# The state-space path of a hybrid encoder block: input tables on VectorE, one real prefix scan for the chunk states, output tables made late and kept in SBUF

## The reference, cut to what matters

```python
lam_bar = exp(lam * dt)                      # 64 groups x 64 complex states
b_bar   = ((lam_bar - 1) / lam)[..., None] * (b_re + 1j * b_im)
bu      = einsum('gpc,bsgc->bsgp', b_bar, u)             # 16 channels per group
states  = associative_scan(a_r*a_l, a_r*b_l + b_r)       # over 256 tokens
y = einsum('gcp,bsgp->bsgc', c_re, real(states)) - einsum('gcp,bsgp->bsgc', c_im, imag(states))
y = gelu(y + d_skip * u);  y = rmsnorm(y * sigmoid(y @ w_glu + b_glu))
```

## Time and profile before

| what | value |
|---|---|
| median of 3 runs | 1181.74 us (1181.29 to 1186.13) |
| profiled execution, its own time | 1184.79 us |
| its span, first to last instruction | 1182.9 us |
| PE busy | 1146.3 us (97%) |
| DVE busy | 743.5 us (63%) |
| ACT busy | 519.8 us (44%) |
| POOL busy | 174.9 us (15%) |
| mean granted TensorE clock | 0.985 |

### The profile page before, as it was taken

The page is one execution under the profiler, slowest core; times in us unless marked ns, Lnnn a source line. Parts: engine busy times, 40 slices in busy tenths (PEclk is TensorE's granted clock), DMA queues, the critical chain, the costliest instruction groups (busy, mean ns, idle before and its releaser), DMA issues.

```text
span 1182.9 us, 15345 instructions
## 1 busy us (share of the span) xinstructions
PE 1146.3 (97%) x5616; PEld 946.1 (80%) x5616; DVE 743.5 (63%) x844; ACT 519.8 (44%) x590; POOL 174.9 (15%) x197
## 2 busy tenths in 40 slices
PE   9879999899999999999999999999999999999996
PEld 6667778677898888888888888888888888888884
DVE  6999998764585565446465555546464555556465
ACT  6533343434574465343434344343434343343443
POOL 7464550884010000000000000000000000000000
PEclk9889899999999999999999999999999999999998
DMA  9577479869565656666666665666666665656652
GB/s 366 194 207 198 152 225 198 269 213 249 180 214 185 193 176 214 206 185 194 187 189 192 195 192 182 194 189 191 187 195 184 190 195 190 191 185 195 187 187 89
DMA packets 147401, 233.74 MB, mean 198 GB/s; under 512 B 25824, under 2 KB 46048, under 8 KB 146592
## 3 DMA queue, kind: packets, MB, share of 16 engines
q1 hardware_dynamic: 146432, 231.75, 64.8%
q0 software_dynamic: 640, 1.31, 0.5%
q10 hardware_dynamic: 288, 0.13, 0.0%
HBM read 223.82 MB, written 8.32 MB: 196 GB/s over the span
## 4 chain that ended last, share of the span: by engine, by line
PE 83%; DVE 8%; SPq 3%; DMA 3%; ACT 1%; issue 1%; POOL 1%; ACTq 0%; POOLq 0%; DVEq 0%
PE ps L1227 26%; PE ps L1229 25%; PE ps L1228 25%; DVE w_lo L746 3%; DMA raw<-in_w_in 3%; SPq L307 1%; DVE cl L887 1%; PE ps L1438 1%; SPq L344 1%; DVE cl_t L888 1%; PE ps L1507 1%; PE ps L1509 1%; PE ps L1508 1%; PE ps L1349 1%; PE ps L1306 1%
## 5 line engine op out<-in xcount | busy, mean ns | idle before, releaser
L746 DVE TENSOR_TENSOR w_lo<-raw,w_hi 128x1024 fp32r<-128x1024 f32 x384 | 486.4, 1271 | 403.0 <-ACT w_hi L468 402.1
L468 ACT ACTIVATE w_hi<-raw 128x1024 fp32r<-128x1024 f32 x384 | 407.0, 1061 | 643.8 <-PE ps L1229 545.2
L1227 PE MATMUL ps<-w_hi,actA_hi 128*128 128x512 f32 x576 | 230.2, 400 | 2.9 <-DVE w_lo L746 2.9
L1229 PE MATMUL ps<-w_hi,actA_lo 128*128 128x512 f32 x576 | 225.0, 391 | 0.0
L1228 PE MATMUL ps<-w_lo,actA_hi 128*128 128x512 f32 x576 | 224.8, 390 | 0.0
L1229 PE MATMUL ps<-w_hi,h2B_lo 128*128 128x512 f32 x352 | 137.0, 389 | 0.0
L1228 PE MATMUL ps<-w_lo,h2B_hi 128*128 128x512 f32 x352 | 136.9, 389 | 0.0
L1227 PE MATMUL ps<-w_hi,h2B_hi 128*128 128x512 f32 x352 | 136.9, 389 | 0.0
L1227 PEld LDWEIGHTS ps<-w_hi,actA_hi 128*128 128x128 f32 x576 | 108.5, 188 | 27.5 <-issue 4.9
L1229 PEld LDWEIGHTS ps<-w_hi,actA_lo 128*128 128x128 f32 x576 | 108.4, 188 | 23.0
L1228 PEld LDWEIGHTS ps<-w_lo,actA_hi 128*128 128x128 f32 x576 | 108.6, 189 | 20.6
(11 more groups left out here) (204 smaller groups left out, 1164.0 us busy)
## 6 DMA issues: line engine op xcount, KB each, us to landing
raw<-in_w_gate SPq DMA_DIRECT2D x88, 512.0 KB, 3.6
raw<-in_w_up SPq DMA_DIRECT2D x88, 512.0 KB, 3.7
raw<-in_w_down SPq DMA_DIRECT2D x88, 512.0 KB, 3.8
raw<-in_w_in SPq DMA_DIRECT2D x80, 512.0 KB, 5.5
raw<-in_w_out SPq DMA_DIRECT2D x32, 512.0 KB, 4.6
c_scratch<-cl SPq DMA_DIRECT2D x8, 512.0 KB, 3.4
y_tab<-c_scratch SPq DMA_DIRECT2D x8, 512.0 KB, 6.8
raw<-in_ssm_w_glu SPq DMA_DIRECT2D x8, 512.0 KB, 3.4
```

Of the source, the lines that this page charges most:

```text
L468: nc.scalar.activation(w_hi[:, s % SPL], raw[:, s % RAW], ACT.Copy).then_inc(S["high_done"], 1)
L746: tt(w_lo[:, s % SPL], raw[:, s % RAW], w_hi[:, s % SPL].bitcast(F32), ALU.subtract).then_inc(S["low_done"], 1)
L1227: mm(o, x_hi, h, start=first, stop=False)
L1229: return mm(o, x_lo, h, start=False, stop=last)
```

## The change

- The factor (lam_bar - 1)/lam is taken out of the input tables. `wb_table(b)` on DVE now uses the raw `b_re`, `b_im` (three 128x896 operations; ACT copies the ninth part), `bb` and `bbx` are gone, and `input_factors` multiplies the factor into the powers after the last input table, so that the output tables carry it.
- `angle_table`, `turn_tables` (ACT: four 128x1024 activations) make sines and cosines of each group's angle times the time chunk. `scan_states` turns the chunk inputs by them, does one real prefix scan with the moduli (`tensor_tensor_scan`, 128x1024) and `turn_back` turns back, per half of the groups. Each turn needs a copy with the halves swapped: `swap`, two DMAs of 256 KB, before the scan and again after it.
- The output tables `cl` are made later (`CL_AT` 31 to 60), stay in SBUF in three buffers and are read there by PE; only the in-chunk kernels go through DRAM (`k_table`: one store, its landing awaited, eight strips back into two buffers).
- `tables` is split: `wb_transposes` at `TR_AT`, `k_tables` at `K_AT`. The outputs come one batch at a time at chunks 39 to 70.
- POOL does no table and no scan any more; it issues the DMAs of the path (`u_local`, `swap`, `k_table`), which stood in SP's program before. `c_dram` and the second copy of u are gone.

```diff
-U_TR = (12, 21)
-CL_AT = (17, 19, 22, 25, 28, 31, 34, 37)
-TAB_AT = (16, 19, 25, 28, 31, 34, 37, 40)
-V_AT = tuple(t + 5 for t in TAB_AT)
-SCAN_AT = tuple(41 + 4 * k // 5 for k in range(NCH - 2))
+U_TR = (12, 19)
+WB_AT = (13, 15, 18, 20, 22, 24, 26, 28)
+TR_AT = (15, 17, 21, 23, 25, 27, 29, 31)
+V_AT = (18, 20, 24, 26, 28, 30, 32, 34)
+ANGLE_AT = (23, 27)
+TURN_AT = (26, 30)
+DECAYS_AT = (27, 34)
+FACTOR_AT = 29
+SCAN_AT = (30, 39)
+BACK_AT = (34, 42)
+CL_AT = (31, 35, 40, 45, 48, 53, 56, 60)
+K_AT = (33, 37, 42, 47, 50, 55, 58, 62)
+Y_AT = (39, 43, 48, 53, 56, 64, 67, 70)
-Y_AT = (64, 65, 67, 68, 70, 71, 73, 74)
-Y1T_MM = (70, 72, 77, 79)
+Y1T_MM = (68, 70, 73, 75)
...
+            def wb_table(b):
...
+                o, t = wb[b % 3][:, :, 1:], wb_t[:, :, 1:]
+                tt(o, of_groups(b_re, b, LOC - 1), of_powers(pr, b, 1, LOC - 1), ALU.mult)
+                link(tt(t, of_groups(b_im, b, LOC - 1), of_powers(pi, b, 1, LOC - 1), ALU.mult))
+                tt(o, o, t, ALU.add).then_inc(S["wb_ready"], 1)
...
+            def scan_states(h):
+                dve.wait_ge(d_swap[h], 32)
+                dve.wait_ge(S["turn_step"], 4 * h + 4)
+                dve.wait_ge(S["decays_ready"], h + 1)
+                x, y = (flat(z) for z in state_half(h))
+                tt(y, y, flat(sin[h][:]), ALU.mult)
+                link(tt(x, x, flat(cos[h][:]), ALU.mult))
+                link(tt(x, x, y, ALU.add))
+                nc.vector.tensor_tensor_scan(x, flat(decays[:]), x, 0.0, ALU.mult, ALU.add).then_inc(S["scanned"], 1)
+
+            def turn_back(h):
+                dve.wait_ge(S["scanned"], h + 1)
+                dve.wait_ge(d_swap_back[h], 32)
+                x, y = (flat(z) for z in state_half(h))
+                tt(y, y, flat(sin[h][:]), ALU.mult)
+                link(tt(x, x, flat(cos[h][:]), ALU.mult))
+                tt(x, x, y, ALU.subtract).then_inc(S["state_ready"], 1)
...
+            def k_table(b):
+                pool.wait_ge(S["kst_ready"], b + 1)
+                pool.dma_start(k_dram[b].rearrange("h p w -> p h w"), kst[:, b % 2]).then_inc(d_kst[b % 2], 16)
+                pool.wait_ge(d_kst[b % 2], 16 * (b // 2 + 1))
...
+                if b >= TBUF:
+                    pool.wait_ge(S["y_mm"], b - TBUF + 1)
+                for i in range(LOC):
+                    pool.dma_start(k_tab[i * CH:(i + 1) * CH, b % TBUF],
...
+            for h in range(2):
+                u_local(h)
+            for h in range(2):
+                pool.wait_ge(S["v_free"], HB * (h + 1))
+                swap(h, d_swap)
+            for h in range(2):
+                pool.wait_ge(S["scanned"], h + 1)
+                swap(h, d_swap_back)
+                k_table(h)
+            for b in range(2, 6):
+                k_table(b)
...
-                pe.wait_ge(S["v_free"], NB)
+                pe.wait_ge(S["y1_ready"], sum(bank == 7 for bank in Y_BANK))
```

More of the change, by code:

```diff
@@ L294, in build, with state_half, flat @@
         kst_w = kst[:].rearrange("p u h (d c) -> p u h d c", c=CH)
[L296 to L325, removed]
+        def state_half(h):
+            at = slice(HALF * h, HALF * (h + 1))
+            return state[:, at], swapped[:, at]
+        def flat(x):
+            return x.rearrange("p g k -> p (g k)")
         @block.sync
@@ new lines, in angle_table @@
+            def angle_table(h):
+                if h == 0:
+                    dve.wait_ge(S["uT_mm"], 2)
+                else:
+                    dve.wait_ge(d_uTst[1], 16)
+                c, s = cos[h], sin[h]
+                link(tt(c[:], scr[:, 2, HALF * h:HALF * (h + 1)].unsqueeze(2).to_broadcast([P, HALF, NCH]),
+                        vec[:, V_COUNT:V_COUNT + NCH].unsqueeze(1).to_broadcast([P, HALF, NCH]), ALU.mult))
+                link(ts(flat(s[:]), flat(c[:]), MAGIC, None, ALU.add))
+                stt(flat(c[:]), flat(s[:]), -MAGIC, flat(c[:]), ALU.add, ALU.subtract).then_inc(S["angles_ready"], 1)
@@ new lines, in wb_transposes @@
+            def wb_transposes(b, part):
+                if part == 1:
+                    pe.wait_ge(S["wb_ready"], b + 1)
+                    pe.wait_ge(S["wb0_ready"], b + 1)
+                    pe.wait_ge(S["u_copied"], 1 if TR_AT[b] < U_TR[1] else 2)
+                    if b:
+                        pe.wait_ge(S["wbT_ready"], b)
+                for g in range(4 * (part - 1), 4 * part):
+                    ins = tr(ps[:, 4 + g // 4, P * (g % 4):P * (g % 4 + 1)],
+                             wb[b % 3][:, g].rearrange("p d c -> p (d c)"), ident[:])
+                if part == 2:
+                    ins.then_inc(S["wb_mm"], 1)
@@ new lines, in k_tables @@
+            def k_tables(b):
+                pe.wait_ge(S["cl_ready"], b + 1)
+                if b == 0:
+                    pe.wait_ge(S["b_pad_ready"], 1)
+                else:
+                    pe.wait_ge(S["kpsum_free"], b)
+                for g in range(BG):
+                    h, q = divmod(g, 4)
+                    gg = BG * b + g
+                    ins = mm(ps[32 * q:32 * q + 32, 6, P * h:P * (h + 1)],
+                             b_re[:, gg:gg + 2].rearrange("p a c -> p (a c)"),
+                             cl[:, b % CBUF, g, 0:LOC].rearrange("p d c -> p (d c)"), start=True, stop=True)
+                ins.then_inc(S["k_mm"], 1)
@@ new lines, in y_batch @@
+            def y_batch(b):
+                pe.wait_ge(S["state_ready"], b // HB + 1)
+                pe.wait_ge(d_ktab[b % TBUF], 16 * LOC * (b // TBUF + 1))
+                if b:
+                    pe.wait_ge(S["y1_ready"], b)
+                else:
+                    pe.wait_ge(S["v_free"], NB)
+                if Y_BANK[b] == 6:
+                    pe.wait_ge(S["kpsum_free"], NB)
+                for a in range(2):
+                    at = slice(P * a, P * (a + 1))
+                    for q in range(4):
+                        mm(ps[32 * q:32 * q + 32, Y_BANK[b], at], u_loc[:, BG * b + 4 * a + q],
+                           k_tab[:, b % TBUF, 4 * a + q], start=True, stop=False)
+                    for q in range(4):
+                        ins = mm(ps[32 * q:32 * q + 32, Y_BANK[b], at], state[:, BG * b + 4 * a + q],
+                                 cl[:, b % CBUF, 4 * a + q, 1:].rearrange("p d c -> p (d c)"),
+                                 start=False, stop=True)
+                ins.then_inc(S["y_mm"], 1)
```

432 lines of the change are left out of this document (201 added, 231 removed).

## The result

The changed kernel takes 1189.66 us (median of 14 runs, 1186.29 to 1191.02) against 1183.68 us before (14 runs, 1181.29 to 1188.08). The ratio is 1.0043, with a 95% interval of 1.0032 to 1.0053 (it is worked out from all the runs and is not the ratio of the two medians, which would be 1.0051): slower, by about the 0.5% that the prediction called no change. Forecast were 1171.5 us and a range up to 1185. The profiled execution has a span of 1187.8 us, 4.9 us more than before.

What follows compares the result with a forecast made beforehand. TensorE bounds the kernel, busy 97%; chunks 0 to 79 lose 36 us, mostly to late VectorE. Old 36 less new losses 25.8 gives gain 10.2: 1184.8 to 1174.6, 1171.5 as a median, range 1161 to 1185.

Steps and rivals of the forecast that it cites:

- What goes away: Chunks 0 to 79: VectorE's operations turn short, losses at parameters, first `cl` and scans go; all of the old 36 us.
- Chunks 12 to 14: Chunk 12 starts in time, but `wb_table(0)` at 13 makes `low(14)` late for TensorE: loss 1.7 us.
- The way of u: Store and strips of u land at 66 us, TensorE wants them in chunk 18 at 63: loss 3, bounds 0 and 15.
- The scan, 2.4 us: Chunks 18 to 33: scan operation taken as two passes, VectorE's lead shrinks to about 1: loss 0.5 us, bounds 0 and 3.
- Chunk 34: TensorE idles after chunk 34 while VectorE awaits a queued swap: 12 us, bounds 11 and 15.5, plus 2.6 of slow clock.
- The output batches: From chunk 39, batches 0, 1 and 2 arrive late by 2.6, 1.6 and 0.6 us; slow clock beside these waits 1.2.
- Chunks from 80 on as before: From about chunk 80 only TensorE's own work counts and the change touches none of it: no difference there.
- rival 1: Output tables' strips land after 7 us instead of 3 in five batches: 1183 to 1186 us, no measurable change; chance 0.20.
- Rival 2: GpSimd's issue cost grows with a DMA's rows, 2.2 us each, first chunk inputs 15 us later: 1188 us; chance 0.10.
- Rival 3: Waits besides chunk 34 do not appear, u and strips land in time: gain 21 us, 1161 us; chance 0.12.
- The trap of GpSimd's issues: GpSimd's 80-odd DMA issues beside busy VectorE are not slowed; single-input passes of `angle_table` might add 1 us at most.

Runs made afterwards that it cites:

- e2: Kernel after the change with the first two batches of chunk inputs two chunks later (V_AT 20, 22 instead of 18, 20): 1180.80 us, ratio 0.9968 against before.
- e5: Kernel after the change with the first three output batches later (Y_AT begins 41, 44, 49 instead of 39, 43, 48): 1188.81 us, ratio 1.0027 against before.
- e3: Kernel after the change with small tiles moved so that matmul operands begin at multiples of 512 bytes in SBUF: 1181.97 us, ratio 0.9981 against before.
- e1: Kernel after the change with GpSimd issuing half 0's swap back before half 1's swap: 1174.32 us, ratio 0.9916 against before.

## Why the prediction was wrong, step by step

- *What goes away:* right. `w_lo` at 1.22 us, no VectorE operation of 3 us, no wait on the first `cl`, no new wait from chunk 54 on. (A slip of no consequence: 6 x 0.75 is 4.5 and not 4.4.)
- *Chunks 12 to 14:* nearly. Chunk 14 takes 3.97 us, 1.25 over 2.72, for a forecast loss of 1.7; another 0.9 is lost at chunk 10, which I did not see.
- *The way of u:* **mis-sized**, 3 us forecast, 9.1 measured (e2). The last strip landed at 67.7 us for a forecast 66, the smaller part of it, and that it came so close is luck: the store began at 49.5 for 51 and took 5.6 for 6.4, and the strips took 12.4 from first issue to last landing for 8.2. The larger part: I had taken one term of 1.2 us for the slow clock beside all waits but that of chunk 34, though the earlier trace rows had priced one wait of 4.5 us at 2.5, and here the clock stood at half for 9.4 us behind a wait of 4.4.
- *The scan, 2.4 us:* 2.29 measured, loss at chunks 30 to 32 none. But chunk 25 lost 1.4 us (5.55 for 4.12), behind TensorE's wait of 1.3 for ACT's copy `wbT`, which my walk did not have. The Trainium skill (DVE: opcode table, instruction layouts, handler registers and perf-mode slots, section "Datapath and trigger behaviour") has the built-in prefix scan at half throughput; the trace agrees, 2.29 us beside 1.22 for a product of the same size.
- *Chunk 34:* right, mechanism and size. 12 us of wait were forecast and 12.5 measured; with the clock behind it 14.6 against 15.1 to 15.5. The last swap was issued 3.2 us behind chunk 34 for 3.4 and landed 4.8 later for 3.4, inside its bounds.
- *The output batches:* right in kind, **mis-sized**. Batch 0 lost 7.7 us in chunk 39 (11.62 against the 3.97 of an undisturbed one) for 2.6 and a share of the 1.2: the addition was done 19.1 us behind chunk 34 for 18.5, the store took 5.6 us from issue to landing and not 4, the last strip landed 4.0 after its issue for 3.1, and the half clock lasted from 172.7 to 179.6 us. Batches 1 and 2 lost nothing, for 1.6 and 0.6: the pause at batch 0 gave the others their lead. Treating the three as a sum was the error; e5 shows that they share one debt of VectorE.
- *"Chunks from 80 on as before":* **wrong**, the step that turned "no change" into slower. 6.3 us are lost from chunk 124 on; without them (e3) the ratio is 0.9981, with 1 inside its interval. The full diff had the line `sb("to_512", [P, 96])` among the removed ones, and I gave addresses no term and no reason for leaving it out.
- *The rivals:* rival 1 had five batches late by slow landings; one batch was late, and the strips of the first five batches landed after 2.3 to 4.5 us. Rival 2 falls, since GpSimd's strips of u took 0.63 us each and those of `k_tab` 0.53. Rival 3 falls, since both waits that it left out appeared, 4.4 us for u and 5.1 for batch 0.
- *The trap of GpSimd's issues:* it did not spring. The earlier trace rows show the eight issues but not what VectorE did beside them, so that part of the reading had no row. In the kernel after, eight issues took 4.21 us at 166.32 while VectorE ran its second scan, a `w_lo` and a `cl` product. The single-input pass of `angle_table` took 0.69 us and not 1.2, and met no issue, so no run here tests whether such a pass holds one up.

The sum: chunks 0 to 79 gained 1.0 us instead of 10.2, 9.2 too few (6.1 on the way of u, 1.7 at the outputs, 0.9 at chunk 10, 0.5 to 0.9 at the block, less 1 that the scan and chunk 14 did not take; that is 8.2 to 8.6, and with chunk 25, 1.4, and chunk 53, 0.5 (4.47 us for 3.96 in e1), 10.1 to 10.5, so the terms overshoot by about 1 us, which stays open); 6.3 us for the places; and the kernel before itself had a median 1.9 us higher in 14 runs than in the 3 I started from. 1171.5 + 9.2 + 6.3 + 1.9 = 1188.9, against 1189.66.

## What to carry to other kernels

A removed filler is an edit with a price of its own: compare the tiles' addresses before and after, and keep stationary and moving operands at the same place modulo 256 bytes, which is what the five distances tried here say. When several waiting instructions share one queue, put them in the order in which what they wait for comes true, and charge each long wait of TensorE with the half clock behind it: in these traces every wait of 3.1 us or more had some, and the three waits of 0.6, 0.9 and 1.3 us in the kernel after (chunks 10, 14 and 25) had none; of those between 1.9 and 3.0 us in all the runs some had and some had not. Waits that one late engine causes are one debt: removing one of them moves it to the next.

## What the runs showed of the hardware

- Where matmul operands lie against each other in SBUF changes the pace of 128x512 matmuls: 2.72 us for twelve with `h2B` at a distance of 0 or 256 bytes modulo 512 from the weights, 2.79 at 128 or 384 and 2.80 at 64 (88 chunks each).
- How long the half clock (granted 0.50 to 0.53, the lower level of 1.2 GHz) stays behind a wait varies: 9.4 us behind a wait of 4.4 us (67.8 to 77.2), 5.4 behind 12.5 and 5.6 behind 5.1 (the two rows below), 5.4 behind 4.5 in the earlier trace rows.

```profile
153.90:159.30 5.40, 5.37 (x13) 4.15 (x14) 5.37 (x5) 0.00 (x0) 0.00 (x0) 0.52 0.33 97
174.00:179.60 5.60, 5.47 (x41) 4.34 (x42) 5.23 (x6) 0.00 (x0) 1.04 (x2) 0.50 0.84 256
```

- The same 64 KB strip of u landed after 3.3 to 8.0 us. The eight of the first half, 4.8 to 8.0 us, were issued in a stretch in which the DMA engines were 95% busy (first row), those of the second half, 3.3 to 4.0, in one with 74% (second row). Two stretches do not show that the share is the cause:

```profile
50.00:62.00 12.00, 12.00 (x62) 9.87 (x61) 11.90 (x13) 5.75 (x9) 5.46 (x9) 1.00 0.95 275
87.00:95.00 8.00, 8.00 (x43) 6.69 (x42) 6.59 (x7) 4.46 (x6) 4.99 (x8) 1.00 0.74 176
```
